# First weight tile in two units with reordered loads; last two feature tiles and the final norm in token halves

## The chip, the cores and the metric

The kernel runs on one NeuronCore of a Trainium2 chip. The metric is the device time of one execution in microseconds, lower is better. All arithmetic is float32 as the caller sees it: a matrix product is done as three TensorE products of "fp32r" halves (a high part and the rest), which is what the names ending in `h`/`l` and `whi`/`wlo` are.

## What is computed

Two decoder blocks on one sequence of 512 tokens and 1024 features. The first block is a gated linear recurrence (HGRN2), an MLP, a differential attention and a second MLP. The second block has windowed attention, a state-space branch, cross attention, an MLP, and at last a norm over the features. The two ends of the program are what matters here:

```python
h = rms_norm(x, a_norm_pre); proj = h @ a_w_in          # the very first product
...
h = rmsnorm(x, norm_ffn)
x = x + square(relu(h @ w_up)) @ w_down                 # the very last product
return rmsnorm(x, norm_final)                           # x * rsqrt(mean(x*x) + eps) * gain
```

## The kernel before

Activations stand feature-major: `h[128, 8, 512]` holds 8 feature tiles (k = 0 to 7) of 128 features by 512 tokens. `XA`, `XB`, `XC` are operands of the products, each a high part and a low part per feature tile.

**Units.** Weights come in units. A unit is up to 128x1024 numbers: 8 k-tiles of 128 columns, 4 of 256 or 2 of 512. Each unit is loaded by one DMA on the queue of SyncE (SP) into one of three raw buffers (512 KB), ScalarE (ACT) makes `whi` (L2247), VectorE (DVE) makes `wlo` (L2462), and TensorE (PE) multiplies. The load of unit n waits until `wlo` of unit n-3 is made; the split of unit n waits for its load and until PE is done with unit n-3.

**Order.** Every engine walks one list of steps, `p.order`, in program order and blocks on the first step whose semaphore is not there; nothing on an engine overtakes. The list is put together at the end of `make_plan` (L1920 to L1938). Its beginning is written out by hand (L1925): gains, first_warm, load 0, x0, x1, load 1, x2, x3, load 2, x4, x5, two DMAs of constants, x6, x7, split 0, load 3. After that the steps follow as the program emitted them, and ahead of each product step with unit number n the splits up to n+2 are placed (n+3 of them, but only n+2 where n is 0 or 1), each followed by the load three units on (L1932).

**The head** (L879 to L901). For k = 0 to 7 the tile x_k is scaled and split into XB (`xsplit`, ACT L2256 then DVE L2470) and squared (`sq`, ACT L2260) and its square added to a sum (`sq_add` on GpSimd (POOL), L2835; the one of k = 6 on DVE, L2475). After k = 1 and after k = 3 the generator `g0` gives one product step of the value projection: unit 0 (k = 0, 1) and unit 1 (k = 2, 3), 24 matmuls each (L1984 to L1986). Ahead of k = 5 stands `setup`, some small DVE and ACT operations on the constants (L2509 to L2535), which waits for the constants to land. When the loop is over, the f projection of head 0 follows (unit 2, L1978 to L1980, 24 matmuls over k = 0 to 7), then the column sums of the squares by a product with ones (L1997), the factor r (`rfin`, ACT L2268 and L2270) and the q projection (unit 3). The table `tabA` is loaded early and is first read at L2568.

**The tail** (`down_q` for qt = 3 in the last MLP, L993 to L1016, and L1902 to L1917). The last 1024 rows of w_down are multiplied by XC. Feature tiles 0 to 3, then 4 and 5, then 6, then 7 are produced, 24 matmuls of 512 columns for each feature tile. DVE adds a result to h (`mix`, L2486), ACT squares it. Tile 7 is added and squared in two halves of 256 tokens (`mix_halves`, `last_halves`). The sums by ones and `rfin` are in halves too. Then `final` (L2821, DVE) scales h in place: tiles 0 and 1 in halves, tiles 2 to 7 whole, and each tile is stored by a DMA of 256 KB on SP's queue as soon as it is scaled (L2929).

Of the kernel before, what the change touches and what calls it, by code (L numbers as in the profile page):

```python
# [281 lines left out]
def make_plan(nc, io, out_d, es, lens):  # L282
# [30 lines left out]
    def col(c):  # L313
        return cst[:, c:c + 1]
# [16 lines left out]
                     land=loads[-1].land, whi=sig("whi"), wlo=sig("wlo"), unit_free=p.unit_done[n - NW] if n >= NW else NONE)  # L331
        return loads, split

    def gemm(X, nk, name, cols, jobs, evac, k0=0, x0=0, ntok=S, ring=ring_g, gate=None, pack=1, piece=None, halves=False):
# [12 lines left out]
        for kk in range(0, nk, step):  # L347
            n = min(step, nk - kk)
            while any(X.ready[x0 + k] is None for k in range(kk, kk + n)):
                yield WAIT  # L350
            while gate and not piece and kk + step >= nk and not gate():
                yield WAIT
            parts, first = [], len(p.units)
            for x in range(0, n, per):
                u = (name, k0 + kk + x, min(per, n - x), tuple(cols))
                parts.append((tile_of(whi, len(p.units) % NW, u), tile_of(wlo, len(p.units) % NW, u)))
                p.units.append(u)
            if pack > 1 and piece:

                for o in outs:  # L360
                    while gate and o.at == pack - 1 and not gate():
                        yield WAIT
                    d = sig("unit")
                    p.pieces += 1
                    add("unit", n=first, parts=parts, per=per, at=0, nk=n, kk=kk, total=nk, ntok=ntok, outs=[o], done=[d],
                        xh=X.hi, xl=X.lo, x0=x0, x_ready=list(X.ready), ends=True, begins=o.at == 0)
                    if o is outs[-1]:
                        p.unit_done += [d] * len(parts)
                    X.after = [d]
                    if o.at == pack - 1:  # L370
                        p.begin(evac(o.job, o.i // pack, o.bank, d))
                    else:
                        p.advance()
                    yield
                return
            if halves and kk == 0:
                fm = jobs[0][0] == "fm"
                if fm:

                    z = add("zeros", zero=X.lo[:, nk - 1, :], x_free=X.after, banks=taken, filled=sig("zeros.filled"), opened=sig("zeros"))  # L380
                    X.after = X.after + [z.opened]
                    yield
                for x in range(2):
                    done = [sig("unit")] if x else []
                    add("unit", n=first, parts=parts, per=per, at=0, nk=n, kk=0, total=nk, ntok=256, c0=256 * x, outs=outs if fm else outs[2 * x:2 * x + 2], done=done,
                        xh=X.hi, xl=X.lo, x0=x0, x_ready=list(X.ready), ends=False, begins=not fm, opened=fm, late=True)
                    if x:
                        p.unit_done += done * len(parts)
                    yield
                continue  # L390
            for at in range(0, n, piece or n):
                m = min(piece or n, n - at)
                ends = kk + at + m == nk
                while gate and piece and ends and not gate():
                    yield WAIT
                done = [sig("unit") for _ in outs] if ends else [sig("unit")] if at + m == n else []
                if done:
                    p.unit_done += [done[-1]] * len(parts)
                p.pieces += 1
                add("unit", n=first, parts=parts, per=per, at=at, nk=m, kk=kk + at, total=nk, ntok=ntok, outs=outs, done=done,  # L400
                    xh=X.hi, xl=X.lo, x0=x0, x_ready=list(X.ready), ends=ends, begins=kk + at == 0)
                if ends:
                    X.after = [done[-1]]
                    for o, d in zip(outs, done):
                        if o.at == pack - 1:
                            p.begin(evac(o.job, o.i // pack, o.bank, d))
                else:
                    p.advance()
                yield
# [25 lines left out]
    def norm_sum(nk, n=S, by="sq_add", left=1):  # L435
# [16 lines left out]
                st["last"] = st.get("last", []) + [(q, sq, 0, n)]  # L452
            return sq

        def last_halves(srcs, ready):

            q = sqs.take()
            st["last"] = [(q, add("sq", src=s, src_ready=r, q=q, c0=x * 256, n=256, sq=sig("sq")).sq, x * 256, 256) for x, (s, r) in enumerate(zip(srcs, ready))]
            return st["last"][1][1]
        tile.halves = last_halves  # L460

        def half(x, src, ready):

# [68 lines left out]
    def hsrc(k):  # L532
        return h[:, k, :]
# [13 lines left out]
        return r, rt  # L547

    HALVES = slice(0, 256), slice(256, S)

    def mix_halves(mx, bk, m, mx_free, plus):
        return [add("mix", mx=mx[:, c], bank=bk, cols=c, unit=m, mx_free=mx_free, plus=plus, mix=sig("mix")).mix for c in HALVES]

    halves_of_h = {}

    def post_norm(mx, g):

# [136 lines left out]

    with ExitStack() as sc:
        tb = K.tabA = sb("tabA", [P, NM_A], scope=sc)
        add("load_tab", land=sig("tab_in", 16))
        K.tab_in = (p.sems["tab_in"], 16)
        VT = sb("Vg", [P, 4, D], scope=sc)
        held = {"q": 2, "f": 2, "qn": 4, "kn": 4, "gt": 4, "sg": 3}  # L700
        BF = VT[:, :, :].rearrange("p i (a t) -> p (i a) t", a=2)
# [171 lines left out]
        norm = {}  # L873

        def v_gemm(hf):
            return gemm((XB, XA)[hf], 8, "a_w_in", [(2048 + hf * 512, 512)], [("tm", 0, 512)], v_evac(hf), ring=ring_h if hf else ring_g)


        rcol = sb("rcolA", [P, 4], scope=sc)  # L879
# [1 line left out]
        for k in range(8):  # L881
# [2 lines left out]
                K.lam, K.lb, K.eps = s.lam, s.lb, s.eps  # L884
            split(XB, k, hsrc(k), ht[k], scale=col(gain["a_norm_pre"] + k), src2=K.gain_in)
            tile(hsrc(k), ht[k])
            if k in (1, 3):
                next(g0)
        fq0 = fq_gemm(0, ring_a)
        next(fq0)  # L890
# [8 lines left out]
        s1 = add("rcol", bank=b, r=fac0["r"], rfin=fac0["t"], rcol=rcol, scope_free=[], half=True, mm=sig("rcol.mm"), done=sig("rcol"))  # L899
        b.free(s1.done)  # L900
        rcol_ready = s1.done  # L901

        def products():
            r, rt = fac0["r"], fac0["t"]
# [53 lines left out]

    def mlp(up, down, post, begun, squares, ones, nxt, then=None, pre=None, then_ring=ring_all):
        nonlocal end
        with ExitStack() as sc:
            XC = Operand(sb("XCh", [P, 8, S], F32R, scope=sc), sb("XCl", [P, 8, S], F32R, scope=sc), 8)
# [26 lines left out]
                    yield from up_gemm(qt, hf * 4, 4)  # L991

            def down_q(qt):  # L993
                for k0, n in ((0, 4), (4, 4)) if qt < 3 else ((0, 4), (4, 2), (6, 1), (7, 1))[:3 if post is not None else 4]:
                    def evac(j, i, b, m):
                        k = k0 + j[1] // P
                        if qt == 3 and post is not None:
                            yield from evac_p(k, b, m, [at[k]], True)
                            return
                        if qt == 3 and post is None and k == 7:  # L1000
                            halves_of_h[k] = mix_halves(acc[:, k, :], b, m, [at[k]], True)
                            ht[k] = halves_of_h[k][1]
                            b.free(ht[k])
                            nxt(k)
                            yield
# [34 lines left out]
                p.run(down_q(qt))  # L1040
            if post is not None:
                close_p(us[1], down, 24, nxt, then[::2], then_ring, [at[7]], True)
            end = [ht[7], p.unit_done[-1], XA.ready[7] or p.unit_done[-1]] + ([bias["rows"]] if pre else [])

    def some(g, n):
# [853 lines left out]
        end = [ht[7], p.unit_done[-1], XA.ready[7]]  # L1899
    outer.close()  # L1900
    both.close()
    last_tile, last_ones = norm_sum(8)  # L1902

    def last(k):
        if k < 7:
            last_tile(hsrc(k), ht[k])
        else:
            last_tile.halves([h[:, k, c] for c in HALVES], halves_of_h[k])
    mlp("w_up_2", "w_down_2", None, begun, squares, ones, last)
    b = [ring_a.take(), ring_a.take()]  # L1910
    r, rt = rms_close(b, last_ones(b), D)

    for k, x in [(0, 0), (1, 0), (0, 1), (1, 1)] + [(k, 2) for k in range(2, 8)]:
        c = (*HALVES, ALL)[x]
        f = add("final", h=h[:, k, c], gain=col(gain["norm_final_2"] + k), r=r.t[:, c], rfin=rt[x % 2 if x < 2 else 1], h_ready=ht[k], scaled=sig("final"))
        if x:
            add("store", out=out_d[:, k, :], h=h[:, k, :], scaled=f.scaled, land=sig("out", 16))  # L1917


    loads, splits = [], []  # L1920
    for n, u in enumerate(p.units):
        a, b = weight_steps(u, n)
        loads.append(a)
        splits.append(b)
    order = [load_gain, p.order[0]] + loads[0] + load_x[0:2] + loads[1] + load_x[2:4] + loads[2] + load_x[4:6] + [load_cst] + load_x[6:8] + [splits[0]] + loads[NRAW]  # L1925
    placed = 1
    for s in p.order[1:]:
        if s.kind == "unit":
# [1114 lines left out]
```

## Time and profile before

| | us |
|---|---|
| median of 3 runs | 2535.12 (2534.81 to 3506.26) |
| the profiled execution | 2533.52 |
| its span in the profile | 2531.7 |

The span runs from the first instruction that is recorded to the last event. The profiled execution has 1.8 us outside it. A row of a timeline reads: start, duration (both us), engine, line, operation, result<-inputs, shape, count, and in brackets how long the engine had been idle and what released it. Where several rows of one line follow each other they are merged with a count. "ns" durations of matmuls overlap, since matmuls are pipelined: their pace is read from starts. PEclk is the granted clock of TensorE as a share of 2.4 GHz.

### The profile page before, as it was taken

What the parts mean: (1) busy time and instruction counts of PE and PEld (TensorE: products, weight loads), DVE (VectorE), ACT (ScalarE), POOL (GpSimd) and SP (SyncE); (2) the same over time, 40 slices, a digit from 0 to 9 for tenths busy, and PEclk for the clock granted to TensorE, in tenths of its full rate; (3) what the DMA queues carried; (4) which work ended last, traced back from release to release, by engine and by line L of the source; (5) the groups of instructions that cost most, each with busy time, mean ns of one, the idle gap of its engine ahead of it and who ended that gap; (6) DMA issues with size and microseconds to landing.
All of it is one profiled execution on the core that took longest, in us unless ns stands there. A gap on an engine that the chain in (4) does not pass through costs nothing.

```text
span 2531.7 us, 35862 instructions
## 1 busy us (share of the span) xinstructions
PE 2466.2 (97%) x14408; PEld 2008.6 (79%) x14408; DVE 1466.1 (58%) x2366; ACT 1168.2 (46%) x2091; POOL 162.2 (6%) x156
## 2 busy tenths in 40 slices
PE   9999999999999999999999899999999999999998
PEld 6888778888777678888877788887877877888886
DVE  6665554433656564344378898786676556543343
ACT  5354353322456644233257676666455444432232
POOL 2110110000100010000001111111000010100001
PEclk9999999999999999999999999999999999999999
DMA  5222234534322223333324333333322233233322
GB/s 155 76 60 76 59 102 112 131 104 119 95 87 82 67 70 106 92 100 92 99 62 132 100 117 101 109 116 112 110 67 67 96 121 100 78 106 100 95 97 75
DMA packets 201781, 243.42 MB, mean 96 GB/s; under 512 B 8080, under 2 KB 133296, under 8 KB 201360
## 3 DMA queue, kind: packets, MB, share of 16 engines
q1 hardware_dynamic: 201616, 241.12, 32.0%
q8 instruction: 115, 1.88, 0.3%
q14 instruction: 50, 0.41, 0.0%
HBM read 231.00 MB, written 9.57 MB: 95 GB/s over the span
## 4 chain that ended last, share of the span: by engine, by line
PE 79%; DVE 11%; ACT 6%; issue 3%; DMA 1%; POOL 0%; DVEq 0%; SPq 0%; ACTq 0%; POOLq 0%
PE bank L1978 22%; PE bank L1980 22%; PE bank L1979 22%; DVE CV L2687 2%; DVE wlo L2462 2%; PE bank L1984 1%; PE bank L1985 1%; PE bank L1986 1%; PE bank L1997 1%; ACT E L2387 1%; ACT whi L2247 1%; PE bank L2179 1%; PE bank L2187 1%; PE bank L2200 1%; DVE h L2496 1%
## 5 line engine op out<-in xcount | busy, mean ns | idle before, releaser
L2462 DVE TENSOR_TENSOR wlo<-raw,whi 128x1024 fp32r<-128x1024 f32 x389 | 491.2, 1269 | 627.8 <-ACT whi L2247 625.5
L2247 ACT ACTIVATE whi<-raw 128x1024 fp32r<-128x1024 f32 x389 | 406.9, 1053 | 580.3 <-PE bank L1980 568.2
L1978 PE MATMUL bank<-XAh,whi 128*128 128x512 f32 x1552 | 615.4, 397 | 6.4 <-DVE XAl L2470 3.4
L1980 PE MATMUL bank<-XAh,wlo 128*128 128x512 f32 x1552 | 601.6, 388 | 0.0
L1979 PE MATMUL bank<-XAl,whi 128*128 128x512 f32 x1552 | 601.5, 388 | 0.0
L1978 PEld LDWEIGHTS bank<-XAh,whi 128*128 128x128 f32 x1552 | 291.6, 188 | 78.8 <-issue 12.1
L1980 PEld LDWEIGHTS bank<-XAh,wlo 128*128 128x128 f32 x1552 | 291.5, 188 | 61.1
L1979 PEld LDWEIGHTS bank<-XAl,whi 128*128 128x128 f32 x1552 | 291.8, 188 | 57.5 <-issue 1.0
L1978 PE MATMUL bank<-XBh,whi 128*128 128x512 f32 (+1 forms) x840 | 331.7, 395 | 1.8 <-DVE XBl L2468 1.6
L1980 PE MATMUL bank<-XBh,wlo 128*128 128x512 f32 (+1 forms) x840 | 324.0, 386 | 0.0
L1979 PE MATMUL bank<-XBl,whi 128*128 128x512 f32 (+1 forms) x840 | 323.7, 385 | 0.0
L2835 POOL TENSOR_TENSOR sum<-sum,sq 128x512 f32<-128x512 f32 (+1 forms) x60 | 78.7, 1312 | 1807.0 <-ACT sq L2260 1801.8
L1978 PEld LDWEIGHTS bank<-XBh,whi 128*128 128x128 f32 x840 | 157.8, 188 | 40.9 <-issue 7.1
L1980 PEld LDWEIGHTS bank<-XBh,wlo 128*128 128x128 f32 x840 | 157.8, 188 | 32.3
L1979 PEld LDWEIGHTS bank<-XBl,whi 128*128 128x128 f32 x840 | 157.9, 188 | 31.6 <-issue 1.0
L1978 PE MATMUL bank<-XCh,whi 128*128 128x512 f32 (+1 forms) x400 | 152.6, 381 | 0.0
L1980 PE MATMUL bank<-XCh,wlo 128*128 128x512 f32 (+1 forms) x400 | 152.2, 381 | 0.0
L1979 PE MATMUL bank<-XCl,whi 128*128 128x512 f32 (+1 forms) x400 | 152.2, 381 | 0.0
L2312 ACT ACTIVATE tmp<-tmp 128x512 f32<-128x512 f32 x96 | 59.7, 633 | 105.4 <-DVE tmp L2591 105.4
L1984 PE MATMUL bank<-whi,XAh 128*128 128x256 f32 (+1 forms) x320 | 105.3, 329 | 2.9 <-DVE XAl L2470 1.5
L1985 PE MATMUL bank<-wlo,XAh 128*128 128x256 f32 (+1 forms) x320 | 101.4, 317 | 0.0
L1986 PE MATMUL bank<-whi,XAl 128*128 128x256 f32 (+1 forms) x320 | 101.4, 317 | 0.0
(330 smaller groups left out, 3255.5 us busy)
## 6 DMA issues: line engine op xcount, KB each, us to landing
raw<-in_w_in SPq DMA_DIRECT2D x77, 512.0 KB, 4.1
raw<-in_up SPq DMA_DIRECT2D x64, 512.0 KB, 3.7
raw<-in_down SPq DMA_DIRECT2D x64, 512.0 KB, 3.8
raw<-in_a_w_in SPq DMA_DIRECT2D x32, 512.0 KB, 4.2
E<-scr_rows SPq DMA_DIRECT2D x32, 512.0 KB, 5.6
raw<-in_w_up SPq DMA_DIRECT2D x32, 512.0 KB, 3.6
raw<-in_w_down SPq DMA_DIRECT2D x32, 512.0 KB, 3.6
raw<-in_w_kv SPq DMA_DIRECT2D x16, 512.0 KB, 3.6
```

What stands on the lines that cost most here:

```text
L1978: pe.matmul(out, wh[:, w, c], xh[:, x, r], start=st, stop=False)
L1979: pe.matmul(out, wh[:, w, c], xl[:, x, r], start=False, stop=False)
L1980: m = pe.matmul(out, wl[:, w, c], xh[:, x, r], start=False, stop=en)
L1984: pe.matmul(out, xh[:, x, r], wh[:, w, c], start=st, stop=False)
L1985: pe.matmul(out, xh[:, x, r], wl[:, w, c], start=False, stop=False)
L1986: m = pe.matmul(out, xl[:, x, r], wh[:, w, c], start=False, stop=en)
L1997: pe.matmul(s.bank.t[:, c], K.ones, s.q.t[:, c], start=s.first, stop=s.final).then_inc(s.ones[0], 1)
L2247: act.activation(s.hi, s.raw, ACT.Copy).then_inc(s.whi[0], 1)
L2312: act.activation(s.t.t[:, :], s.t.t[:, :], ACT.Square).then_inc(s.up[0], 1)
L2462: dve.tensor_tensor(s.lo, s.raw, s.hi.bitcast(F32), ALU.subtract).then_inc(s.wlo[0], 1)
L2687: m = dve.scalar_tensor_tensor(out=cv[:, o], in0=x[:, i], scalar=w, in1=cv[:, o], op0=ALU.mult, op1=ALU.add)
L2835: pool.tensor_tensor(t, t, s.q.t[:, 0:s.n], ALU.add).then_inc(s.added[0], 1)
```

## The change

At the head: the first call of `gemm` gets `fine=2`: its first two k-tiles are units of their own (units 0 and 1, 256 KB each), and k = 2, 3 are unit 2. `g0` is advanced after k = 0, 1 and 3. So the f projection becomes unit 3, q becomes unit 4, and so on by one. The hand-written order of loads changes: x1 follows load 1, x2 to x5 follow load 2, then comes load 3, and x6, x7 and the constants stand behind it. The load of `tabA` moves behind the step `rcol`.

At the tail: tiles 6 and 7 are no longer made by `down_q` but by `finish`. Each is made for tokens 0 to 255 first and for tokens 256 to 511 later, so there are four products of 24 matmuls with 256 columns. Norm, scaling and store of the first half of the tokens stand between the products of the second half. The stores are of half-tiles: two of 512 KB for the first half, four of 256 KB for the second.

```diff
-    def gemm(..., halves=False):
+    def gemm(..., halves=False, fine=0):
...
-        for kk in range(0, nk, step):
-            n = min(step, nk - kk)
+        for kk in [*range(fine), *range(fine, nk, step)]:
+            n = 1 if kk < fine else min(step, nk - kk)
...
+        tile.sum, tile.added = lambda: st["sum"], lambda: st["added"]
...
-        add("load_tab", land=sig("tab_in", 16))
-        K.tab_in = (p.sems["tab_in"], 16)
...
-            return gemm(..., v_evac(hf), ring=ring_h if hf else ring_g)
+            return gemm(..., v_evac(hf), ring=ring_h if hf else ring_g, fine=0 if hf else 2)
...
             tile(hsrc(k), ht[k])
-            if k in (1, 3):
+            if k in (0, 1, 3):
                 next(g0)
...
         rcol_ready = s1.done
+        add("load_tab", land=sig("tab_in", 16))
+        K.tab_in = (p.sems["tab_in"], 16)
...
-                for k0, n in ((0, 4), (4, 4)) if qt < 3 else ((0, 4), (4, 2), (6, 1), (7, 1))[:3 if post is not None else 4]:
+                for k0, n in ((0, 4), (4, 4)) if qt < 3 else ((0, 4), (4, 2), (6, 1))[:3 if post is not None else 2]:
...
+    def finish(X, name, k0):
+        u = [(name, k0, 8, ((k * P, P),)) for k in (6, 7)]
...
+        def product(i, x, lo=0, hi=8):
+            done = [sig("unit")] if hi == 8 else []
+            add("unit", n=n0 + i, parts=parts[i:i + 1], per=8, at=lo, nk=hi - lo, kk=lo, total=8, ntok=256, c0=256 * x, ...)
...
+            ht[6 + i] = e = add("mix", mx=h[:, 6 + i, c], bank=bs[i][x], cols=c, unit=done[0], mx_free=[at[i]], plus=True, mix=sig("mix")).mix
+            sq[i, x] = add("sq", src=h[:, 6 + i, c], src_ready=e, q=qs[i], c0=x * 256, n=256, sq=sig("sq")).sq
...
+        product(0, 0)
+        product(1, 0)
+        for x in range(2):
+            ones_of(last_tile.sum(), last_tile.added(), x, first=True)
+        product(0, 1, 0, 4)
+        ones_of(qs[0], sq[0, 0], 0)
+        factor(0, ones_of(qs[1], sq[1, 0], 0, final=True))
+        scale(0, (0, 1))
+        product(0, 1, 4, 8)
+        store(0, 0, 4, scale(0, (2, 3)))
+        product(1, 1, 0, 4)
+        ones_of(qs[0], sq[0, 1], 1)
+        store(0, 4, 4, scale(0, (4, 5, 6, 7)))
+        product(1, 1, 4, 8)
+        factor(1, ones_of(qs[1], sq[1, 1], 1, final=True))
+        for k in range(0, 8, 2):
+            store(1, k, 2, scale(1, (k, k + 1)))
...
-    order = [load_gain, p.order[0]] + loads[0] + load_x[0:2] + loads[1] + load_x[2:4] + loads[2] + load_x[4:6] + [load_cst] + load_x[6:8] + [splits[0]] + loads[NRAW]
+    order = [load_gain, p.order[0]] + loads[0] + load_x[0:1] + loads[1] + load_x[1:2] + loads[2] + load_x[2:6] + [splits[0]] + loads[NRAW] + load_x[6:8] + [load_cst]
```

`ones_of`, `factor`, `scale` and `store` each add one step (or one `final` for each k) for one half of the tokens.

## Rows read from the trace of the kernel before

**Rows 1.** The page: busy time by engine, and the chain that ended last by engine.
```profile
PE 2466.2 (97%) x14408; PEld 2008.6 (79%) x14408; DVE 1466.1 (58%) x2366; ACT 1168.2 (46%) x2091; POOL 162.2 (6%) x156
...
PE 79%; DVE 11%; ACT 6%; issue 3%; DMA 1%; POOL 0%; DVEq 0%; SPq 0%; ACTq 0%; POOLq 0%
```
**Rows 2.** Timeline of the first 28 us: PE, DVE, POOL, ACT, engines mixed.
```profile
8.56 0.47 PE L1984 MATMUL bank<-whi,XBh 128*128 128x512 f32 x1 [1.32 <-DVE XBl L2470]
...
9.52 1.06 ACT L2247 ACTIVATE whi<-raw 128x1024 fp32r<-128x1024 f32 x1 [0.76 <-DMA raw<-in_a_w_in]
...
10.62 1.23 DVE L2462 TENSOR_TENSOR wlo<-raw,whi 128x1024 fp32r<-128x1024 f32 x1 [1.52 <-ACT whi L2247]
...
11.76 0.75 DVE L2470 SCALAR_TENSOR_TENSOR XBl<-h,cst,XBh 128x512 fp32r<-128x512 f32 x1
...
16.37 1.78 DVE L2470 SCALAR_TENSOR_TENSOR XBl<-h,cst,XBh 128x512 fp32r<-128x512 f32 x1
18.08 0.22 DVE L2513 TENSOR_TENSOR lwork<-cst 128x64 f32<-128x64 f32 x1
...
20.30 1.30 POOL L2835 TENSOR_TENSOR sum<-sum,sq 128x512 f32<-128x512 f32 x1 [2.70 <-ACT sq L2260]
...
20.32 1.30 DVE L2535 TENSOR_TENSOR lbt<-lbt 128x8 f32<-128x8 f32 x1
...
23.47 0.74 DVE L2470 SCALAR_TENSOR_TENSOR XBl<-h,cst,XBh 128x512 fp32r<-128x512 f32 x1
...
24.29 0.48 PE L1978 MATMUL bank<-XBh,whi 128*128 128x512 f32 x1
...
25.08 1.02 PE L1997 MATMUL bank<-sum,cst 128*128 128x512 f32 x2
```
**Rows 3.** Timeline of SP's queue: issue of loads 0, 3 and the table.
```profile
1.18 0.42 SPq L2877 DMA_DIRECT2D raw<-in_a_w_in  x1
...
9.73 0.53 SPq L2877 DMA_DIRECT2D raw<-in_a_w_in  x1
10.30 2.72 SPq L2886 DMA_DIRECT2D tabA<-in_tabA  x1
```
**Rows 4.** DMA view of loads 0 and 3 alone: KB, us from issue to landing.
```profile
raw<-in_a_w_in SPq DMA_DIRECT2D x1, 512.0 KB, 4.2
...
raw<-in_a_w_in SPq DMA_DIRECT2D x1, 512.0 KB, 8.9
```
**Rows 5.** First use of the table by DVE, timeline.
```profile
55.05 0.73 DVE L2568 COPY_PREDICATED SCt<-tabA,bank 128x256 f32<-128x256 int32 x1
```
**Rows 6.** Busy time by stretch, two neighbours (last three columns: PEclk, DMA share, GB/s).
```profile
1295.50:1298.90 3.40, 1.21 (x6) 0.74 (x5) 3.40 (x5) 3.26 (x5) 0.00 (x0) 1.00 0.00 0
1298.90:1302.40 3.50, 3.50 (x11) 2.73 (x10) 3.50 (x6) 0.29 (x1) 0.00 (x0) 0.56 0.76 202
```
**Rows 7.** PE's timeline around those stretches.
```profile
1298.51 0.47 PE L1984 MATMUL bank<-whi,XBh 128*128 128x512 f32 x1 [2.19 <-DVE wlo L2462]
```
**Rows 8.** PE's timeline where half-wide matmuls and products with ones alternate.
```profile
657.64 0.28 PE L1978 MATMUL bank<-XCh,whi 128*128 128x256 f32 x1
...
661.96 0.60 PE L1997 MATMUL bank<-sum,cst 128*128 128x256 f32 x2
...
662.94 0.28 PE L1979 MATMUL bank<-XCl,whi 128*128 128x256 f32 x1
```
**Rows 9.** Timeline of the last 12 us, engines mixed.
```profile
2520.24 0.76 DVE L2486 TENSOR_TENSOR h<-bank,h 128x256 f32<-128x256 f32 x2 [3.36 <-PE bank L1980]
...
2522.86 5.67 DVE L2821 SCALAR_TENSOR_TENSOR h<-h,cst,rr 128x256 f32<-128x256 f32 x10 [1.86 <-ACT rr L2270]
```
**Rows 10.** Chain that ended last, one of its last pieces (start, us, what).
```profile
2524.55 3.98 DVE h L2821 x6
```
**Rows 11.** Source view of the stores: min, median, max to landing.
```profile
DMA to landing us min/median/max: 2.1/2.4/2.5
```
**Rows 12.** PE's busy time by stretch over tiles 6 and 7 before.
```profile
2509.32:2520.20 10.88, 10.88 (x50) 9.01 (x49) 2.08 (x3) 1.26 (x2) 1.33 (x2) 1.00 0.01 2
```

More of the change, by code:

```diff
@@ L332, in weight_steps, with gemm @@
         return loads, split
-    def gemm(X, nk, name, cols, jobs, evac, k0=0, x0=0, ntok=S, ring=ring_g, gate=None, pack=1, piece=None, halves=False):
+    def gemm(X, nk, name, cols, jobs, evac, k0=0, x0=0, ntok=S, ring=ring_g, gate=None, pack=1, piece=None, halves=False, fine=0):
         width = sum(c[1] for c in cols)
@@ L453, in tile @@
             return sq
[L455 to L460, printed above, removed]
+        tile.sum, tile.added = lambda: st["sum"], lambda: st["added"]
         def half(x, src, ready):
@@ L549, in make_plan @@
     HALVES = slice(0, 256), slice(256, S)
-    def mix_halves(mx, bk, m, mx_free, plus):
-        return [add("mix", mx=mx[:, c], bank=bk, cols=c, unit=m, mx_free=mx_free, plus=plus, mix=sig("mix")).mix for c in HALVES]
-    halves_of_h = {}
     def post_norm(mx, g):
@@ L875, in v_gemm @@
         def v_gemm(hf):
-            return gemm((XB, XA)[hf], 8, "a_w_in", [(2048 + hf * 512, 512)], [("tm", 0, 512)], v_evac(hf), ring=ring_h if hf else ring_g)
+            return gemm((XB, XA)[hf], 8, "a_w_in", [(2048 + hf * 512, 512)], [("tm", 0, 512)], v_evac(hf), ring=ring_h if hf else ring_g, fine=0 if hf else 2)
         rcol = sb("rcolA", [P, 4], scope=sc)
@@ L957, in make_plan, with mlp @@
         end = [ht[7], p.unit_done[-1], XA.ready[7], XB.after[0]]
-    def mlp(up, down, post, begun, squares, ones, nxt, then=None, pre=None, then_ring=ring_all):
+    def mlp(up, down, post, begun, squares, ones, nxt, then=None, pre=None, then_ring=ring_all, finish=None):
         nonlocal end
@@ L998, in evac @@
                             yield from evac_p(k, b, m, [at[k]], True)
[L999 to L1005, printed above, removed]
                             return
@@ L1042, in mlp @@
                 close_p(us[1], down, 24, nxt, then[::2], then_ring, [at[7]], True)
+            else:
+                finish(us[1], down, 24)
             end = [ht[7], p.unit_done[-1], XA.ready[7] or p.unit_done[-1]] + ([bias["rows"]] if pre else [])
@@ L1901, in make_plan @@
     both.close()
[L1902 to L1917, printed above, removed]
+    last_tile, _ = norm_sum(8)
@@ new lines, in finish, with ones_of, factor, scale @@
+    def finish(X, name, k0):
+        u = [(name, k0, 8, ((k * P, P),)) for k in (6, 7)]
+        n0 = len(p.units)
+        parts = [(tile_of(whi, (n0 + i) % NW, u[i]), tile_of(wlo, (n0 + i) % NW, u[i])) for i in range(2)]
+        p.units.extend(u)
+        bs = [[ring_all.take() for _ in range(2)] for _ in range(2)]
+        rb, r, qs = [ring_all.take() for _ in range(2)], rrs.take(), [sqs.take() for _ in range(2)]
+        at, sq, rt = [ht[6], ht[7]], {}, [None, None]
+        def product(i, x, lo=0, hi=8):
+            done = [sig("unit")] if hi == 8 else []
+            p.pieces += 1
+            add("unit", n=n0 + i, parts=parts[i:i + 1], per=8, at=lo, nk=hi - lo, kk=lo, total=8, ntok=256, c0=256 * x,
+                outs=[Step(job=("fm", 0), i=0, bank=bs[i][x], at=0)], done=done, xh=X.hi, xl=X.lo, x0=0, x_ready=list(X.ready), ends=bool(done), begins=lo == 0)
+            if not done:
+                return
+            if x:
+                p.unit_done.append(done[0])
+            c = HALVES[x]
+            ht[6 + i] = e = add("mix", mx=h[:, 6 + i, c], bank=bs[i][x], cols=c, unit=done[0], mx_free=[at[i]], plus=True, mix=sig("mix")).mix
+            bs[i][x].free(e)
+            sq[i, x] = add("sq", src=h[:, 6 + i, c], src_ready=e, q=qs[i], c0=x * 256, n=256, sq=sig("sq")).sq
+        def ones_of(q, sq, x, first=False, final=False):
+            return add("ones", q=q, sq=sq, bank=rb[x], c0=x * 256, n=256, first=first, final=final, ones=sig("ones")).ones
+        def factor(x, m):
+            rt[x] = add("rfin", bank=rb[x], ones=m, r=r, c0=x * 256, n=256, dim=D, rfin=sig("rfin")).rfin
+            rb[x].free(rt[x])
+        def scale(x, ks):
+            c = HALVES[x]
+            for k in ks:
+                f = add("final", h=h[:, k, c], gain=col(gain["norm_final_2"] + k), r=r.t[:, c], rfin=rt[x], h_ready=ht[k], scaled=sig("final"))
+            return f.scaled
+        def store(x, k, n, scaled):
+            add("store", out=out_d[:, k:k + n, HALVES[x]], h=h[:, k:k + n, HALVES[x]], scaled=scaled, land=sig("out", 16))
+        product(0, 0)
[15 more added lines that the diff above has]
+            store(1, k, 2, scale(1, (k, k + 1)))
@@ L1920, in make_plan @@
+    mlp("w_up_2", "w_down_2", None, begun, squares, ones, lambda k: last_tile(hsrc(k), ht[k]), finish=finish)
     loads, splits = [], []
```

## The prediction

> **What bounds the kernel now.** I read the page first: TensorE is busy for 97% of the span and holds 79% of the chain that ended last [rows 1]. So nearly every microsecond between the first product and the last is PE work at a fixed pace, and a change at the ends can win only what lies before the first product, behind the last one, or in gaps of PE. Then I read the timeline of the first 28 us by engine, with the queue of SP and the landing of each load beside it, and last the timeline of the final 12 us.
>
> At the head PE's first real product starts at 8.56, released by the low part of x0 [rows 2]. From there PE runs without a gap to the end of the f projection at 25.08, where the product with ones starts [rows 2]. What the reader should see is how little slack there is: the low part of x7 is begun at 23.47 for 0.74 us, ends at 24.21, and PE's matmul on it starts at 24.29 [rows 2]. PE and the chain that makes x4 to x7 arrive together. That decides this change: starting PE earlier gives nothing unless the chain behind x7 comes earlier too.
>
> At the tail PE is done with tile 7 at 2520.20 [rows 12], DVE adds the two halves of tile 7 at 2520.24, the first `final` starts at 2522.86 and DVE scales for 5.67 us until 2528.53 [rows 9]. The stores land 2.1 to 2.5 us after issue [rows 11]; the span ends 3.17 us after DVE's last operation.
>
> **Head, what it does to PE's start.** Load 0 is issued at 1.18 and lands 4.2 us later [rows 3, 4]. Half the bytes land earlier and take half of ACT's 1.06 and DVE's 1.23 us [rows 2]. I take 0.4 to 0.7 us for the transfer and about 0.5 us on each engine: PE starts some 1.5 us earlier, near 7.0. It then does unit 0 (12 matmuls), unit 1 (12) and unit 2 (24). The pace of full-width matmuls is 10.88 us for the 48 of tiles 6 and 7, 0.227 us each [rows 12], so 48 take 10.9 us and PE reaches the f projection near 18.
>
> **Head, what the order does to ACT.** This is the term that carries the forecast. The placing rule puts the splits up to n+2 ahead of product step n. Before, unit 2 was the f projection, behind all of the x loop, so splits 3 and 4 stood behind x7. Now unit 2 is the product emitted after k = 3, so splits 3 and 4 stand on ACT and DVE between x3 and x4. ACT may not touch x4 until load 4 has landed. Load 4 is issued behind loads 0 to 3, all x tiles and the constants. Add the sizes in the order of the queue: gains 61 KB, loads 0 and 1 as two halves, loads 2 and 3, 8 x tiles of 256 KB, constants of 256 and 320 KB, and then load 4 with 512 KB make 4,733 KB. Before, load 3 closes exactly the same 4,733 KB. It was issued at 9.73 and landed 8.9 us later, at 18.63 [rows 3, 4]. The queue is full then (the table's DMA behind it was held 2.72 us in issue [rows 3]), so bytes ahead, not distance, set its landing. I take 18.6 for load 4.
>
> From there step by step. ACT makes whi 4 from 18.63; DVE's wlo starts 1.10 later, as 9.52 to 10.62 shows; x4's low part starts 1.14 after that (10.62 to 11.76) and takes about 0.7, giving 21.6 for the first operation of `setup` [rows 2]. The square of x4 is handed to POOL at the same moment. Where POOL adds, DVE's operation is longer: 1.78 instead of 0.75 for the low part of x4, and 1.30 for L2535 on 8 columns, beside POOL's 1.30 at 20.30 [rows 2]. That is 1.1 us. It may fall here or not; I take it, as POOL's add always becomes due here, and keep zero as the other end. Setup starts at 22.7 (21.6). Before, from the first operation of setup at 18.08 to the end of x7's low part at 24.21 were 6.13 us [rows 2], all on DVE behind ACT in the same order as after. So x7 is ready at 28.8 (27.7), and with 25.08 minus 24.29 for its three matmuls the f projection ends at 29.6 (28.5), against 25.08. **Head: +4.5 us, lower bound +3.4.** Later DVE has wlo 3 and wlo 4 behind it already, but the ones product and r, which come next, waited for PE before, so that gives nothing. Behind split 4 on ACT also wait the squares, and for them the sum and r: they are in the same chain, not beside it. If load 4 landed at 17.5 or 19.5, the term moves by as much.
>
> The x6, x7 loads and the constants shift by less than 2 us and are due only after 21 now, so they are covered. The table is first read at 55.05 [rows 5]; moved behind `rcol` its issue comes behind load 9, which by the placing rule goes out about two units (11 us at the pace above) after the ones at 29.6, near 41, and its use is not before 55. Nothing. Without that cover DVE would wait at L2568 and PE behind it.
>
> **Head, the clock.** PE now has x0 to x3 done near 20.9, does x4 for 0.7, then stands until x5 is there, more than 3 us, and does one tile at a time. Where PE stood 2.19 us [rows 7] and was busy 1.21 of 3.4 us, the granted clock of the next stretch was 0.56 of 2.4 GHz, so mostly at 1.2 GHz, and it held only 11 matmuls in 3.5 us [rows 6], where the warm pace gives 15. That is about 1.6 us with some of it perhaps spent waiting. I take 1.0, ends 0 and 3 (two such stretches).
>
> The Trainium skill (TensorE: Matmul & The Clock Gate, "HAM oscillation — how this bites in real kernels") says that a wait for a DMA between bursts makes the next burst start at the low clock. By that rule the whole 1.6 would be paid instead of 1.0.
>
> **Tail.** Before, the 48 full matmuls take 10.88 us [rows 12]. After, 96 half-wide ones at 0.120 us (36 from 657.64 to 661.96 [rows 8]) take 11.52: +0.64. Five products with ones now lie ahead of the last matmul. Two of them and the restart took 661.96 to 662.94, less one matmul 0.86 us [rows 8]. Two pairs and a single one (0.5) are +2.2. None of them waits by my reckoning: DVE's queue (two `final`, `mix` of tile 6, two and then four `final`) is done just as the last product ends, so the `mix` of tile 7 may be up to 0.3 us late. Sum +2.9. From the `mix` to the first `final` it is the same chain as before, 2.62 us (2520.24 to 2522.86) [rows 9]. Then eight halves instead of 5.67 us: four halves took 2522.86 to 2524.55, 0.42 each [rows 9, 10], so 3.4 us, -2.3. Last store: 256 KB in rows half as long, less load on the queue before it; nothing, ends -0.3 and +0.5 by the spread of landings [rows 11]. **Tail: +0.6 us (0.2 to 1.4).** The halves move work ahead of the last matmul, but the products with ones that used to be covered behind it now lie on PE.
>
> **Sum.** 4.5 + 1.0 + 0.6 = +6.1 us. Profiled execution: span 2531.7 to 2537.8, time 2533.5 to 2539.6. The median stands 1.6 above the profiled execution, so 2535.1 + 6.1 = 2541.2. The forecast's own range, with its ends 3.4 + 0 + 0.2 and 5.5 + 3 + 1.4, is 2538.7 to 2545.
>
> **Rivals.**
>
> *Load 4 lands in time (12%).* If the landing of load 4 were set by its own size, ACT would not stand behind split 4 and the x chain would be bounded by the constants alone. For it: load 0 with nothing ahead took 4.2 us [rows 4]. Issued near 9.7 it would be there at 14. Against it: 8.9 us for the same place in the queue. The point of decision is a landing before about 14.5, when ACT comes free from split 3. Then PE's 1.5 us of earlier start count in full: -1.5 + 0.6 = -0.9, 2534.2, faster than before.
>
> The Trainium skill (DMA: Bandwidth & Descriptors, "Anatomy of one DMA — SWDGE (gpsimd) path") gives 2.0 us plus bytes over 436 GB/s for a DMA of the gpsimd path, 3.2 us for 512 KB. By that rule the load would be there at 13, this rival's case, but the 8.9 us of the trace speak against it for a full queue.
>
> *The stall is short (10%).* POOL doesn't collide and the chain runs faster than I read, so that the head costs 2 us and the clock holds: about +2.5, 2537.6. Speaks for it: the 1.1 us is a collision whose timing I only estimate.
>
> *The low clock lasts (10%).* PE stays at 1.2 GHz for two or three stretches, through the ones and q: +4.5 + 4 + 0.6 = +9, 2544 to 2547. For it: between 20.9 and 28.8 PE works only on x4, x5 and x6, about 2 of 7.9 us. Against it: only one such stretch is in my rows, and it is followed by the warm pace within 3.5 us [rows 6].
>
> *The tail gains (5%).* If the ones hid in the pipeline and the 256-wide stores cost nothing, the tail would win up to 1.6 us, and with the head's gain the time would be 2532 to 2534. The measured pace of both speaks against it [rows 8].
>
> **How the numbers follow.** Forecast 63%, rivals 12, 10, 10 and 5%. The range from 2534.5 to 2545.5 leaves out most of the first and last rival and the far end of the long clock: some 2 in 10. The 2% limit is 50 us, about what can be told from no change; all cases are within it, 98%, with 1% on each side for what I have not seen.
>
> **What would show it.** Right: ACT idle between split 3 and split 4 with the DMA of raw as releaser until about 18.6; x4 split behind it; PE idle in the f projection, first ones near 29.6; a granted clock under 1.00 between 24 and 33; the last `mix` about 14 us after tile 6's first matmul instead of 10.9; eight halves of `final` of 0.42. Wrong: x4's high part before 15, or ones before 25.

## The result and the profile after

| | before | after |
|---|---|---|
| median, us | 2535.13 | 2541.71 |
| profiled execution, us | 2533.52 | 2540.05 |
| its span, us | 2531.7 | 2538.3 |
| ratio after/before | | 1.0026 (95% interval 1.0018 to 1.0033) |

The change costs 6.6 us, on a forecast of 6.1. That is far below 2%, but the interval of the ratio lies clear of 1. One of the 13 runs of each kernel took far longer (3506.26 and 6326.97 us) and is not in the ratio.

The page of the kernel after shows that PE's work is what it was, plus 4 us (busy 2466.2 before [rows 1]); the span grew by 6.6:

```profile
span 2538.3 us, 35975 instructions
...
PE 2470.3 (97%) x14460; PEld 2013.0 (79%) x14460; DVE 1466.6 (58%) x2373; ACT 1168.6 (46%) x2093; POOL 160.9 (6%) x156
```

**The head.** ACT's timeline of the kernel after, around the splits of unit 3 (13.91) and unit 4 (18.57). L2277 is the old L2247, L2286 the old L2256:

```profile
12.10 0.62 ACT L2290 ACTIVATE sq<-h 128x512 f32<-128x512 f32 x1
13.91 1.07 ACT L2277 ACTIVATE whi<-raw 128x1024 fp32r<-128x1024 f32 x1 [1.19 <-DMA raw<-in_a_w_in]
18.57 1.06 ACT L2277 ACTIVATE whi<-raw 128x1024 fp32r<-128x1024 f32 x1 [3.59 <-DMA raw<-in_a_w_in]
19.53 0.71 ACT L2286 ACTIVATE XBh<-h,cst 128x512 fp32r<-128x512 f32 x1
```

ACT stands 3.59 us with a DMA as releaser, and x4 is behind it in program order. DVE and POOL of the same kernel:

```profile
19.66 1.23 DVE L2492 TENSOR_TENSOR wlo<-raw,whi 128x1024 fp32r<-128x1024 f32 x1 [3.33 <-ACT whi L2277]
20.80 0.75 DVE L2500 SCALAR_TENSOR_TENSOR XBl<-h,cst,XBh 128x512 fp32r<-128x512 f32 x1
20.84 1.85 POOL L2865 TENSOR_TENSOR sum<-sum,sq 128x512 f32<-128x512 f32 x1 [6.19 <-ACT sq L2290]
21.47 1.30 DVE L2543 TENSOR_TENSOR lwork<-cst 128x64 f32<-128x64 f32 x1
...
27.92 0.74 DVE L2500 SCALAR_TENSOR_TENSOR XBl<-h,cst,XBh 128x512 fp32r<-128x512 f32 x1
```

L2543 is setup's first operation, on 64 columns. It took 0.22 us before [rows 2] and 1.30 here, beside POOL's addition, which is recorded from 20.84 to 22.69. The last row is the low part of x7: ready at 28.66. PE in the f projection, and its busy time in three stretches of it (the third number from the end is the granted clock):

```profile
22.39 0.39 PE L2010 MATMUL bank<-XBh,wlo 128*128 128x512 f32 x1
26.79 0.54 PE L2008 MATMUL bank<-XBh,whi 128*128 128x512 f32 x1 [4.01 <-DVE XBl L2500]
...
29.26 0.63 PE L2008 MATMUL bank<-XBh,whi 128*128 128x512 f32 x1
...
30.53 1.02 PE L2027 MATMUL bank<-sum,cst 128*128 128x512 f32 x2
```
```profile
23.00:26.00 3.00, 0.00 (x0) 0.00 (x0) 2.63 (x13) 2.73 (x7) 1.22 (x1) 1.00 0.44 132
...
26.00:27.10 1.10, 0.32 (x1) 0.30 (x2) 1.10 (x3) 1.10 (x3) 0.04 (x1) 1.00 0.00 0
27.10:30.50 3.40, 3.40 (x9) 2.63 (x8) 2.69 (x4) 0.81 (x1) 0.00 (x0) 0.50 0.02 5
```

PE waits 4.01 us for x5 and resumes at 26.79. From 27.1 to 30.5 the granted clock is 0.50: 1.2 GHz, and a tile takes 1.28 us (27.98 to 29.26) instead of 0.68. The product with ones starts at 30.53 against 25.08 [rows 2]: the head costs 5.45 us.

These 5.45 us divide cleanly. The low part of x4 starts at 20.80 instead of 16.37, 4.43 us later. From there to the product with ones are 9.73 us instead of 8.71, and this 1.0 us more lies between the end of x7's low part and the product with ones (28.66 to 30.53, before 24.21 to 25.08). POOL's addition is no part of the loss: before, it lengthened the low part of x4 (1.78 us), here it lengthens the first operation of setup. The stretch of low clock lasts 3.4 us, which at half the clock is 1.7 us of PE's work; some 0.7 of it pass while x7 isn't ready anyway.

**The tail.** DVE's timeline of the kernel after. L2516 is the addition to h, L2851 the scaling. The first row is the addition of tile 5; the second fence has the same addition in the kernel before:

```profile
2515.81 0.69 DVE L2516 TENSOR_TENSOR h<-bank,h 128x512 f32<-128x512 f32 x1 [2.03 <-PE bank L2010]
...
2525.68 0.88 DVE L2851 SCALAR_TENSOR_TENSOR h<-h,cst,rr 128x256 f32<-128x256 f32 x2 [3.70 <-ACT rr L2300]
2526.48 0.42 DVE L2516 TENSOR_TENSOR h<-bank,h 128x256 f32<-128x256 f32 x1
2526.82 2.46 DVE L2851 SCALAR_TENSOR_TENSOR h<-h,cst,rr 128x256 f32<-128x256 f32 x6
2529.56 0.42 DVE L2516 TENSOR_TENSOR h<-bank,h 128x256 f32<-128x256 f32 x1 [0.29 <-PE bank L2010]
2532.18 3.26 DVE L2851 SCALAR_TENSOR_TENSOR h<-h,cst,rr 128x256 f32<-128x256 f32 x8 [2.19 <-ACT rr L2300]
```
```profile
2509.36 0.69 DVE L2486 TENSOR_TENSOR h<-bank,h 128x512 f32<-128x512 f32 x1 [2.03 <-PE bank L1980]
```

From tile 5's addition to the last one are 13.75 us; before, to the pair of tile 7, 10.88 (2509.36 to 2520.24 [rows 9]): +2.87. From there to the first scaling 2.62, as before. Scaling 3.26 instead of 5.67: -2.41. From its end (2535.44) to the end of the span 2.86 instead of 3.17: -0.31. Sum +0.15 us. The tail is a draw: what left the end of the program came back as products on PE. This length repeats well: from tile 5's addition to the end of the span are 22.45 to 22.47 us in every profiled execution with this tail (after, e1, e3, e6, e7), 22.32 before.

**Between them.** The kernel after runs 5.45 us late at the end of the head and 6.45 us late at tile 5's addition. The missing 1.0 us arises in the middle, in code that the change doesn't touch. Weight splits of equal work, compared one by one, run 5.5 us late at 407 us, 4.9 at 2021, 5.6 at 2044 and 6.45 from 2087 on. The last step, 0.85 us, can be seen in the trace. Here is the same stretch of the program, first before, then after:

```profile
2084.00:2088.00 4.00, 4.00 (x35) 4.00 (x34) 3.31 (x5) 2.98 (x5) 0.00 (x0) 1.00 0.38 125
```
```profile
2089.00:2093.00 4.00, 4.00 (x18) 2.96 (x18) 2.21 (x3) 2.03 (x4) 0.00 (x0) 0.60 0.21 76
```

The granted clock falls in the kernel after and in no other of the profiled executions at this place. The step between 2021 and 2044 (0.7 us) stands in every other run too, at 0.3 to 1.4 us against the one profiled execution of before, so it tells nothing of the change.

### The profile page after: what moved, and what is told of

It reads as the page before. It is cut to its first block, busy times and chain, and to the rows that moved or that the text cites. A ratio compares the mean times of both kernels' runs of the same rounds, so it can differ in the third digit from the quotient of the medians.

```text
span 2538.3 us, 35975 instructions
## 1 busy us (share of the span) xinstructions
PE 2470.3 (97%) x14460; PEld 2013.0 (79%) x14460; DVE 1466.6 (58%) x2373; ACT 1168.6 (46%) x2093; POOL 160.9 (6%) x156
## 3 DMA queue, kind: packets, MB, share of 16 engines
q8 instruction: 115, 1.88, 0.3%
## 4 chain that ended last, share of the span: by engine, by line
PE 80%; DVE 11%; ACT 6%; issue 3%; SPq 0%; DMA 0%; POOL 0%; DVEq 0%; ACTq 0%; POOLq 0%
PE bank L2008 23%; PE bank L2009 22%; PE bank L2010 22%; DVE CV L2717 2%; DVE wlo L2492 1%; PE bank L2014 1%; PE bank L2027 1%; PE bank L2016 1%; PE bank L2015 1%; PE bank L2209 1%; ACT whi L2277 1%; DVE h L2526 1%; PE bank L2217 1%; PE bank L2230 1%; PE bank L2122 1%
## 5 line engine op out<-in xcount | busy, mean ns | idle before, releaser
L2492 DVE TENSOR_TENSOR wlo<-raw,whi 128x1024 fp32r<-128x1024 f32 (+1 forms) x390 | 490.2, 1263 | 629.0 <-ACT whi L2277 626.6
L2277 ACT ACTIVATE whi<-raw 128x1024 fp32r<-128x1024 f32 (+1 forms) x390 | 407.2, 1051 | 583.9 <-PE bank L2010 568.6
L2717 DVE SCALAR_TENSOR_TENSOR CV<-bank,convh,CV 128x510 f32<-128x510 f32 (+1 forms) x128 | 95.7, 748 | 10.5 <-ACT CV L2392 7.1
```

Source lines behind the costliest of these rows:

```text
L2277: act.activation(s.hi, s.raw, ACT.Copy).then_inc(s.whi[0], 1)
L2492: dve.tensor_tensor(s.lo, s.raw, s.hi.bitcast(F32), ALU.subtract).then_inc(s.wlo[0], 1)
L2717: m = dve.scalar_tensor_tensor(out=cv[:, o], in0=x[:, i], scalar=w, in1=cv[:, o], op0=ALU.mult, op1=ALU.add)
```

## Experiments

The runs of one group shared their runs of the kernel before, with medians of 2534.71 (e1 to e4), 2534.96 (e5 to e8) and 2534.90 (e9). "Ones" is the start of the head's first product with ones, read from PE's timeline: 25.08 before and 30.53 after.

| kernel | ones | span | median | ratio to before (95%) |
|---|---|---|---|---|
| e1_tail_only | 24.84 | 2531.7 | 2534.63 | 0.9999 (0.9991 to 1.0008) |
| e2_head_only | 30.85 | 2538.7 | 2540.93 | 1.0024 (1.0015 to 1.0034) |
| e3_split4_late | 24.95 | 2532.6 | 2534.80 | 1.0001 (0.9992 to 1.0010) |
| e4_fill | 29.69 | 2539.7 | 2540.99 | 1.0024 (1.0014 to 1.0033) |
| e5_both | 24.46 | 2531.9 | 2534.33 | 0.9996 (0.9987 to 1.0005) |
| e6_load4_early | 26.74 | 2535.5 | 2537.28, one run | |
| e7_add4_dve | 30.20 | 2538.6 | 2540.38, one run | |
| e8_tail7 | 25.79 | 2533.2 | 2534.70 | 0.9997 (0.9989 to 1.0006) |
| e9_adds_dve | 23.96 | 2531.8 | 2533.81 | 0.9997 (0.9988 to 1.0006) |

### Which end costs: e1 and e2

e1 is the kernel after with the head's edits taken back, e2 the kernel before with the head's edits alone:

```diff
 # e1_tail_only, against after; the load of tabA moves back too
...
-            return gemm(..., fine=0 if hf else 2)
+            return gemm(..., fine=0)
...
-            if k in (0, 1, 3):
+            if k in (1, 3):
...
-    order = [...] + loads[0] + load_x[0:1] + loads[1] + load_x[1:2] + loads[2] + load_x[2:6] + [splits[0]] + loads[NRAW] + load_x[6:8] + [load_cst]
+    order = [...] + loads[0] + load_x[0:2] + loads[1] + load_x[2:4] + loads[2] + load_x[4:6] + [load_cst] + load_x[6:8] + [splits[0]] + loads[NRAW]
```

> The kernel after with its head undone: units, order of loads and the table's load as before; only the tail in token halves remains. Stall theory: the head of before returns, first ones product at 25.1 us, no idle of ACT on split 4, no stretch of low clock in the first 50 us. The tail keeps its 2.87 us of added PE work, 2.4 us less scaling and 0.3 us less at the last store: +0.2 us (0 to 0.8) against the kernel before, so 2535.3. Rival (the tail is the cost, the head is harmless): 5 us or more above before.

> The kernel before with the change of the head alone. Stall theory: ACT idle some 3.6 us until load 4 lands at 18.6, first ones product at 30.5, one stretch of low clock between 26 and 31; +6 us (5 to 7) against before, about 2541.3. Rival (the tail is the cost): within 1 us of before or 1.5 us faster.

e1 is at 0.9999 of before, e2 at 1.0024. In e1 the tail has the lengths of the kernel after (additions from 2509.26 to 2523.01, 13.75 us, and scaling 3.25), and the span is 2531.7, that of before. The head is the whole loss, as far as the intervals tell (about 2 us each way). e2 shows the same wait of ACT, and in its head the same 9.75 us from x4's low part to the product with ones:

```profile
18.86 1.06 ACT L2247 ACTIVATE whi<-raw 128x1024 fp32r<-128x1024 f32 x1 [3.58 <-DMA raw<-in_a_w_in]
```

### The placing of one split: e3

```diff
-            while placed < min(s.n - bool(s.get("late")) + (NW if s.n > 1 else 2), len(splits)):
+            while placed < min(s.n - bool(s.get("late")) + (NW if s.n > 2 else 2), len(splits)):
```

> The kernel after with one number changed in the placing rule: ahead of the product step of unit 2 only split 3 is placed, split 4 goes behind the x loop (ahead of the f projection). Loads, units and tail stay. Stall theory: ACT goes on with x4 at about 15, x7 is ready when the constants and the setup allow, some 23 to 24, first ones product between 23.8 and 25.2, no low clock there; total 5.5 to 7 us below the kernel after, 2534 to 2536. Rival (the order of the loads is the cost: x6, x7 and the constants come too late behind load 3): first ones product stays above 28 and the time above 2539. Rival 2 (units of one k-tile cost PE): same as rival 1.

One number gives the whole loss back: 1.0001 of before. ACT, DVE and PE of e3:

```profile
13.93 1.06 ACT L2277 ACTIVATE whi<-raw 128x1024 fp32r<-128x1024 f32 x1 [1.26 <-DMA raw<-in_a_w_in]
14.89 0.71 ACT L2286 ACTIVATE XBh<-h,cst 128x512 fp32r<-128x512 f32 x1
...
16.18 1.86 DVE L2500 SCALAR_TENSOR_TENSOR XBl<-h,cst,XBh 128x512 fp32r<-128x512 f32 x1
...
24.15 0.50 PE L2008 MATMUL bank<-XBh,whi 128*128 128x512 f32 x1 [0.26 <-DVE XBl L2500]
```

x4's high part starts at 14.89 instead of 19.53. Loads and units are those of the kernel after, so neither the order of the loads nor the small units cost by themselves. But the head gains nothing either: ones at 24.95, 0.13 before that of before, though PE began 1.3 us earlier (7.27 against 8.56). PE waits for x7 (the last row). The chain that makes x4 to x7 didn't move: x4's low part starts at 16.18 against 16.37, behind split 3, for whose load ACT waited 1.26 us (the first row), and from there to ones are 8.77 us against 8.71.

### Bytes ahead in the queue, or a load's own time: e6

```diff
-    order = ... + loads[NRAW] + load_x[6:8] + [load_cst]
+    order = ... + loads[NRAW] + loads[NRAW + 1] + load_x[6:8] + [load_cst]
...
-                if placed + NRAW < len(loads):
+                if 1 < placed < len(loads) - NRAW:
```

> The kernel after with load 4 directly behind load 3 in SP's queue, ahead of x6, x7 and the constants. Theory that the bytes ahead in the queue set the landing: 3,645 KB up to load 4 instead of 4,733, so it lands at 15.0 to 15.7, ACT's wait for it ends then; the constants now close 4,733 KB and land near 18.6, which holds setup; first ones product between 25.5 and 27. Rival (a load has its own fixed time of 8 to 9 us from issue): landing stays above 17.

Split 4 begins at 15.75, released by the DMA after 0.70 us of waiting, where 15.0 to 15.7 was expected, and ones at 26.74. The landing follows the bytes ahead. Load 4 went out at 8.31 here and landed 7.4 us later, so a fixed 8 to 9 us from issue does not fit; but as its issue moved too (10.27 in the kernel after), the two rules lie only 0.6 to 1.5 us apart in this run. The constants were not the next bound: they landed at 18.58, as expected, and setup began at 19.79, right behind x4's low part. It is a single run, and is read by its trace alone.

```profile
15.75 1.06 ACT L2277 ACTIVATE whi<-raw 128x1024 fp32r<-128x1024 f32 x1 [0.70 <-DMA raw<-in_a_w_in]
```

### The collision with GpSimd: e7 and e9

e7 moves one addition of the kernel after, that of k = 4, from POOL to DVE:

```diff
-  st["added"] = add(by if i < nk - 2 else "sq_add_v", ...)
+  st["added"] = add(by if i < nk - 2 and not (own and i == 4) else "sq_add_v", ...)
...
-        g0, (tile, ones) = v_gemm(0), norm_sum(8)
+        g0, (tile, ones) = v_gemm(0), norm_sum(8, own=True)
```

> The kernel after with the sum of the squares of k = 4 of the head made by VectorE instead of GpSimd. Collision theory (VectorE's next operation is held while GpSimd adds; 1.1 us): the first operation of setup takes 0.2 us again instead of 1.30, the addition itself costs 0.6, so the first ones product comes 0.5 us earlier than in the kernel after, near 30.0. Rival (L2543 was long for another reason, the addition is simply more work): ones 0.6 us later, near 31.1.

```profile
20.70 0.74 DVE L2500 SCALAR_TENSOR_TENSOR XBl<-h,cst,XBh 128x512 fp32r<-128x512 f32 x1
21.36 0.69 DVE L2505 TENSOR_TENSOR sum<-sum,sq 128x512 f32<-128x512 f32 x1
21.97 0.22 DVE L2543 TENSOR_TENSOR lwork<-cst 128x64 f32<-128x64 f32 x1
```

L2543 is back at 0.22 us. There is more work on DVE, and yet from the start of x4's low part to the end of x7's are 7.37 us instead of 7.86: 1.1 us of waiting went, 0.6 of addition came. That it is DVE waiting for POOL is shown; by which resource the two exclude each other is not shown by these runs. Ones came 0.33 us earlier, not 0.5; in e7 the low clock lasted into the ones product, whose two parts started 1.70 us apart (30.20 and 31.90) instead of 0.86. This too is a single run.

e9 is e5 (below) with all five additions moved. In its rows L2494 makes the low parts:

> The kernel e5_both with all sums of squares of the head (k = 1 to 5) made by VectorE, so that GpSimd adds nothing there. Collision theory: the low parts of x3 and x4 and the last operation of setup lose 1.1 us each, two additions of 0.6 us come into VectorE's queue ahead of x7; x7 is ready at 23.1 instead of 24.1, PE reaches the f projection near 18.1 and starts the ones product near 23.9 (23.5 to 24.3) instead of 24.5 in e5_both and 25.1 in before. Total 1.9 us below before with the tail's 0.75, 2533.0, ratio 0.9992, at the edge of what the comparison can tell. Rival (the landing of the constants or PE's own start holds the head, not the collisions): ones product at 24.4 or later.

```profile
16.23 0.74 DVE L2494 SCALAR_TENSOR_TENSOR XBl<-h,cst,XBh 128x512 fp32r<-128x512 f32 x1
...
22.36 0.75 DVE L2494 SCALAR_TENSOR_TENSOR XBl<-h,cst,XBh 128x512 fp32r<-128x512 f32 x1
...
18.20 0.39 PE L2002 MATMUL bank<-XBh,whi 128*128 128x512 f32 x1
...
23.96 1.02 PE L2021 MATMUL bank<-sum,cst 128*128 128x512 f32 x2
```

Ones at 23.96, where 23.9 was expected. From the start of x4's low part to ones are 7.73 us; with POOL's additions they are 8.69 to 8.77 in before, e3, e4, e5, e6 and e8. (In e1, 8.11: there only one of POOL's additions lengthened an operation of DVE on this stretch, and PE itself came last, as x7 was ready 1.31 us before ones.) So once split 4 is out of the way two things hold the head at 25: load 3, behind which x4 starts at about 16.2 in e9 too, and POOL's additions behind x4. With the additions gone the head is 1.1 us shorter than before. That takes PE's early start too: in the kernel before PE had no gap from 8.56 to 25.08 and couldn't have been done sooner. The whole kernel is at 0.9997 (0.9988 to 1.0006): 1.1 us below before in the medians, not told apart from no change. Its span of 2531.8 is that of before too: its weight splits run 1.4 us early up to about 1240 us, 0.4 early at 2021, and 0.9 late at 2180.

### What the low clock costs: e4

```diff
...
         next(fq0)                         # f projection, k = 0 to 3
+        b = ring_a.take()
+        s = add("fill", bank=b, x=XB.hi[:, 0, :], n=19, x_ready=XB.ready[3], warm=sig("fill"))
+        b.free(s.warm)
         next(fq0)                         # f projection, k = 4 to 7
...
+            for _ in range(s.n):
+                m = pe.matmul(s.bank.t[:, :], s.x[:, 0:P], s.x, start=True, stop=True)
...
```

> The kernel after with 19 full-width matmuls on data already there (result thrown away, 4.3 us at the warm pace) put on PE between the two halves of the f projection, where PE otherwise waits for x5. They hide in the wait. Clock theory: the granted clock stays at 1.00, the three products of x5 to x7 take 0.7 us each again instead of 1.28, the ones product starts at 29.4 instead of 30.5: 1.1 us (0.8 to 1.5) below the kernel after. Rival (the low clock costs nothing, since PE only waits for x7 anyway): same time within 0.3 us, ones product at 30.5.

```profile
26.00:28.00 2.00, 2.00 (x11) 1.50 (x10) 2.00 (x4) 2.00 (x3) 0.23 (x1) 1.00 0.00 0
...
28.89 0.50 PE L2011 MATMUL bank<-XBh,whi 128*128 128x512 f32 x1 [0.28 <-DVE XBl L2509]
```

The clock stays at 1.00 and ones start at 29.69, 0.84 us earlier than in the kernel after, although x7's low part was ready later by 0.18 (28.10 against 27.92, each for 0.74). So at the head the low clock is worth about 1.0 us. In the whole it didn't show: 1.0024 of before like e2, and the profiled span is 1.4 us above that of after. The weight splits run 4.6 us late at 407 us and 7.9 at 2180 us in this execution. What the middle takes varies from run to run by more than this effect (the runs of e4 alone lie between 2539.29 and 2542.33), so whether the 1.0 us at the head reaches the end is open.

### Another tail: e5 and e8

Tile 6 whole, its square added on DVE, only tile 7 in halves, and the scaling of the first half of the tokens laid into the wait for the second half's norm. e5 has e3's placing, e8 the head of before. The steps of this tail in their order, cut out of the code:

```python
product(0)                                    # tile 7, first half of the tokens
product(1, 0, 3)
ones_of(last_tile.sum(), last_tile.added(), 0, first=True)
factor(0, ones_of(q, sq[0], 0, final=True))
scale(0, (0, 1))
product(1, 3, 8)
ones_of(last_tile.sum(), last_tile.added(), 1, first=True)
store(0, 0, 4, scale(0, (2, 3)))
store(0, 4, 4, scale(0, (4, 5, 6, 7)))
factor(1, ones_of(q, sq[1], 1, final=True))
```

> The placing rule of e3_split4_late, and another tail: tile 6 is made whole as before and its square added on VectorE, only tile 7 is in token halves. PE then has one half-wide product (24), 3 k-tiles, two products with ones, 5 k-tiles ahead of its end: +0.3 us for the half-wide pace and +0.9 for the ones instead of +2.9. The six last scalings of the first half of the tokens lie in the 2.6 us in which the second half's norm is made. By the theory that the products with ones on PE ate the tail's gain: span from tile 6's first matmul to the end 21.3 us instead of 22.5 (after) and 22.4 (before), total 1.1 us below e3_split4_late and before, near 2533.7. Rival (the last stores bound the end, not PE or VectorE): same length as in the kernel after.

> The head of before and the tail of e5_both. Tail theory: 1.1 us below before (0.7 to 1.5), near 2533.6; first ones product of the head at 24.8 to 25.1. Rival (nothing to be had at the tail): 2534.7 within 0.3.

From tile 5's addition (2510.31) to the end of the span (2531.9) e5 takes 21.6 us; before 22.3, after 22.5. Expected was 21.3. DVE's last scaling ends 18.0 us behind that addition, before 19.2, so VectorE's part came as expected (-1.2). Then the stores took part of it back: 3.6 us from there to the end instead of 3.17. The gain of 0.75 us stands in all three executions with this tail (21.57, 21.57 and 21.55 us in e5, e8 and e9, before 22.32). First e5, then before, the DMA view over the stores (the fence of each kernel is its own):

```profile
DMA packets 2144, 2.10 MB, mean 250 GB/s; under 512 B 96, under 2 KB 2144, under 8 KB 2144
...
GB/s 0 0 0 0 29 302 356 341 356 332 361 278 229 346 341 361 327 341 371 327 302 375 351 327 322 375 341 312 351 356 346 337 356 346 190 0 0 0 0 0
```
```profile
DMA packets 1152, 2.10 MB, mean 272 GB/s; under 512 B 128, under 2 KB 128, under 8 KB 1152
...
GB/s 0 0 0 0 0 223 362 372 426 351 362 404 383 383 372 383 362 415 372 383 351 426 372 341 415 404 362 341 415 415 362 362 383 362 32 0 0 0 0 0
```

The same 2.10 MB are 2144 packets in halves and 1152 whole, and flow at about 340 instead of 380 GB/s; in both kernels the DMA engines are busy from the first store to the last. So the rival of that expectation was half right. That the shorter rows make the difference is argued from these two kernels; the stores of e5 also start at other times and two of them are larger. e8 missed: its median is 0.26 us below before, not 1.1, though the interval (0.9989 to 1.0006) leaves room for either. Its profiled execution has ones at 25.79 though its head is that of before. The same head gave 25.08, 24.84 and 25.79 in three kernels, so a start of ones alone, from one execution, is no evidence for differences under 1 us. In e8 the loads explain it: split 1 began at 10.26, released by its load, instead of 9.52 [rows 2], x4's low part started 0.73 us later (17.10), and from there to ones were 8.69 us. Lengths between two points behind the loads repeat far better, and the readings of e4, e7 and e9 rest on those.

## Why the prediction was right

The forecast of the median was 2541.2 us, measured were 2541.71. Step by step, forecast against the kernel after:

| step | forecast | measured |
|---|---|---|
| PE's first product | near 7.0 | 7.14 |
| load 4 landed, split 4 starts | 18.63 | 18.57 |
| first operation of setup delayed by POOL | 1.1, at 21.6 | 1.08, at 21.47 |
| x7 ready | 28.8 | 28.66 |
| price of the low clock | 1.0 | 1.00 (28.66 to 30.53, less the 0.87 of before); e4: about 1.0 |
| head | +5.5 | +5.45 |
| tail, work on PE | +2.9 | +2.87 |
| tail, scaling | -2.3 | -2.41 |
| tail, from the last scaling to the end | 0 | -0.31 |
| tail | +0.6 | +0.15 |
| middle | 0 | +1.0 |
| sum | +6.1 | +6.6 |

**The mechanism was the one named**, and e3 shows it by its cause: one split that needs a late load stood ahead of work that was ready. What made the estimate sharp was not a model of the DMA but a coincidence that could be counted: load 4 after closes the same 4,733 KB as load 3 before. e6 tested the rule behind it at another count of bytes.

**The rival "load 4 lands in time"** had its price wrong. It credited PE's whole early start of 1.5 us to the head. e3, which takes the stall away, gained 0.13 us: x4 waits behind split 3 and its load, the chain from x4 to x7 is as long as before, and x7 is no earlier. The argument had said itself that the early start is worth nothing unless x7 comes earlier, and then did not apply it to the rival. e9 shows that POOL's additions have to go before it is worth 1.1 us.

**Smaller errors.** The forecast took 0.4 to 0.7 us for the transfer of half of load 0; its split began 1.26 us earlier (4.18 against 5.44), and then x0's own transfer came last, so that PE's start near 7.0 came out with wrong parts. PE reached the f projection at 19.22, not near 18. Of this 0.63 us is a wait for x2's low part, which took 1.88 us beside POOL's addition instead of 0.75; the forecast had left out this collision. Another 0.41 us is PE's first matmul, which began at 7.14 while the last warm-up matmul was recorded until 7.71. The late arrival cost nothing, as PE had to wait for x5 anyway. The 1.1 us of POOL's addition was counted as a term that might be absent; the runs show it in the chain before and after alike, in another operation. And the end of the last store came 0.31 us sooner after the last scaling than forecast, at the edge of the stated spread; that the queue was less full then is likely, but not shown.

**The middle is open in part.** 1.0 us arises there in code without a change. 0.85 us of it is one stretch of low clock at 2089 us, in the profiled execution of the kernel after alone. Why it falls there is not known. Such stretches fall at other places in other executions, and e1, e3, e4, e5 and e9 drift by 0.1 to 3.3 us between 407 and 2180 us. That all of this is their placing is argued, not shown, and part of it is at full clock in both traces (2021 to 2044); no run isolates it. So the close agreement of the total is partly luck: the tail was 0.45 too dear, the head 0.05 too dear and the middle 1.0 too cheap.

## What to carry to other kernels

When units of work are renumbered, look at every rule that places work by number: cutting one tile in two moved a weight split four feature tiles earlier in ScalarE's program, and an engine that runs in order stands still for the latest input among what is ahead of it. Before paying for an earlier start, find out which chain arrives last at the point where the work meets, and whether it moves too. Cutting a tail in halves pays only if the extra small products and the shorter DMA rows don't land on the path that they were meant to shorten.

## What the runs showed of the hardware

- A VectorE operation of 0.22 us takes 1.30 when it stands beside GpSimd's addition of 128x512 floats, and 0.22 again when that addition is done by VectorE (e7). With such additions moved, the chain from x4's low part to the product with ones is 1.0 us shorter (7.73 against 8.77) though VectorE does two more additions of 0.6 us in it (e9 against e3).
- Stores of rows of 1 KB flow at some 340 GB/s, of 2 KB at some 380, when the queue is full (e5 and before).
- Behind a wait of 4.01 us PE was granted 1.2 GHz, from 27.1 to 30.5 us. With matmuls whose result nobody reads in that wait it kept 2.4 GHz (e4).
- In a full queue a load's landing followed the bytes issued up to and with it: 4,733 KB had landed at 18.6 us (before), 18.5 (after) and 18.6 (e6) whatever the order, 3,645 KB at 15.2 (after) and 15.7 (e6). In e8 4,733 KB took until 19.4.
